# Expert blocks fed from a DRAM scratch: the row gather per block replaced by one scatter, reads per block, and two combining pairs moved

## The chip, the cores and the metric

The kernel runs on 1 core of one Trainium2 chip. The metric is the device time of one execution in microseconds (us). Engines: PE is TensorE (matmuls; its weight loads are shown as PEld), DVE is VectorE, ACT is ScalarE, POOL is GpSimd, SP is SyncE. A name with q (SPq, POOLq) is an engine's sequencer, the part that issues DMAs and waits. All transfers of the core are carried by 16 DMA engines.

## The reference, cut to what matters

A two-layer step of a model on 288 tokens (256 of a prompt, 32 samples), width 1024, all float32. Each layer mixes tokens (retention heads and a causal convolution) and then runs a mixture of 16 experts, two per token. The change is in the second part:

```python
def grouped_moe(h, w_router, b_router, w_gate, w_up, w_down):
    ...
    wts, local = lax.top_k(cand, TOP_K)            # two experts per token
    wts = wts / jnp.sum(wts, axis=-1, keepdims=True)
    ...
    xs = h_pad[slot_tok].reshape(n_blocks, MOE_BLOCK, D)   # rows of the tokens of each block
    def block_ffn(args):
        xb, e = args
        return (jax.nn.silu(xb @ w_gate[e]) * (xb @ w_up[e])) @ w_down[e]
    ys = lax.map(block_ffn, (xs, block_e)).reshape(cap, D)
    ys = (ys * slot_w[:, None]).astype(h.dtype)
    return jnp.zeros((N + 1, D), h.dtype).at[slot_tok].add(ys)[:N]
```

## The kernel before, in words

**Weights.** Every large weight is streamed once through `ring`, 12 units of 1 MB (L129, `NSLOT`). SP issues the loads in one fixed order. Before each it waits on `freed[s]`, after each the data raises `loaded[s]`. An expert needs exactly 12 units: four of gate, four of up, four of down (L349 to L357). So unit s of expert e+1 is loaded as soon as the last block of expert e has used unit s.

**Blocks.** The tokens of an expert are taken in blocks of 64 slots (`BLK`). An expert with more than 64 assigned tokens runs two blocks (`nsubi`, the inner loop L731), and only its last block lets the ring go on, since `freed` is compared with the count of all blocks. With this data there are 35 blocks for 32 experts: 18 in layer 0, 17 in layer 1.

**One block on PE** (L729 to L788): eight gate products (`half_products`, from `xg`, the transposed rows of the block) with the three combining pairs 0 to 2 of the block before set between k = 3 and k = 4 (`combine`, which writes the block's weighted results back to token order into PSUM); eight up products with pair 3 after k = 0; then `gather`, which picks the rows of the next block out of `h2tok` (288 tokens, in SBUF) by a product with a 0/1 matrix `sel`; the transposes of the hidden row `hs`; the transposes of `selw`; the transposes of the gathered rows `xtok`; then eight down products.

**The other engines.** DVE builds `selw` and `sel` per block (L1388 to L1402), adds what each pair combined to `xT` (`take`, L1377), multiplies gate and up (L1408, L1414), and copies `h2T` and `selT` out of PSUM. ACT takes the sigmoid of the gate, copies the gathered rows (`xtok`, L960), the transposed rows (`xg`, L962) and the result (`ysb`, L965). POOL does nothing between L1546 and L1547, that is during all blocks of a layer.

**Before the first block** of a layer the router runs on DVE (L1285 to L1364, its last result is `slots`, the slot of each token), and the rows of block 0 are gathered on PE from `slot0`, which is known earlier. After the last block come the next layer's first modulation products, whose weights follow the experts' in the ring.

Of the kernel before, what the change touches and what calls it, by code (L numbers as in the profile page):

```python
# [11 lines left out]
T = SEQ + NS  # L12
P = 128
# [8 lines left out]
BLK = 64  # L22
MAXSUB = -(-T // BLK)

MAXBLK = E + (2 * T) // BLK
NC = 1 + B
# [90 lines left out]
def hybrid_step_kernel(nc, x_prompt, x_sample, state_ret, state_conv, c_prompt, c_sample, w_mod, b_mod, g_mix_norm,  # L117
# [6 lines left out]
    with ctx:  # L124
# [20 lines left out]
        nsubi = sb("nsubi", [P, E + 1], i32)  # L145
        rtmp = sb("rtmp", [P, KC, NS])
# [78 lines left out]
        sel1 = cut("moe", 3, BLK)  # L225
# [10 lines left out]
        PAIR_BANKS = ((6, 7), (0, 5), (1, 4), (0, 5))  # L236
# [3 lines left out]
        def sem(name):  # L240
# [4 lines left out]
        in_first, in_const, in_x, in_c, in_rows, in_taps, in_wr = (sem(n) for n in (  # L245
            "in_first", "in_const", "in_x", "in_c", "in_rows", "in_taps", "in_wr"))
        (cpad, cond_step, x_trans, x_copied, x_squared, rows_trans, rows_copied, mod_done, mod_evac,
         fold_done) = (sem(n) for n in (
             "cpad", "cond_step", "x_trans", "x_copied", "x_squared", "rows_trans", "rows_copied",
             "mod_done", "mod_evac", "fold_done"))  # L250
        mix_open, moe_open, y_out, fin_cp = (sem(n) for n in ("mix_open", "moe_open", "y_out", "fin_cp"))
        cb_loaded, routed, x_summed = sem("cb_loaded"), sem("routed"), sem("x_summed")
        tick = sem("tick")
# [7 lines left out]
        dchain pchain sel0_ready g0_done x0_copied gt0_done  # L261
        mod2_done mod2_evac mod2_fold mod2_added""".split()
        moe_names = """sel_ready gathered xrow_copied xg_trans xg_copied
# [13 lines left out]
        fin_rs, fin_y, fin_tr, fin_cd = V.var_ready, V.h_ready, V.h2_trans, V.x_mid  # L277
# [16 lines left out]
        def _(sp):  # L294
# [76 lines left out]
            yp = y_prompt[0].rearrange("(r p) d -> p r d", p=P)  # L371
            sp.wait_ge(fin_cp, 2)
# [11 lines left out]
        def _(pe):  # L384
# [7 lines left out]
            taken = pe.alloc_register("chunks_taken")  # L392
            for s in range(NSLOT):
                pe.sem_inc(freed[s], 1)
# [49 lines left out]
            for j in range(2):  # L444
                mod_slab(j, j, lambda s: 16)
                pe.drain().then_inc(mod_done, 1)
                if j == 0:
                    pe.wait_ge(in_taps, 16)
# [5 lines left out]
                mod_turn(2 + j, modS[:, j, :]).then_inc(fold_done, 1)  # L454
            pe.wait_ge(in_wr, 32)

            for l in range(L):
# [256 lines left out]
                def combine(j):  # L714
                    for hf in range(2):
                        last = mm(ps[:, PAIR_BANKS[j][hf], 0:T], ysb[hf * 64:hf * 64 + 64, j * P:(j + 1) * P],
                                  selT[hf * 64:hf * 64 + 64, :], True, True)
                    return last
# [9 lines left out]
                pe.reg_mov(taken, 2)  # L728
# [845 lines left out]
```

## Time and profile before

| | us |
|---|---|
| median of 3 runs | 1494.03 |
| lowest, highest | 1492.83, 1499.04 |
| the profiled execution | 1498.92 |
| its span | 1497.0 |
| PE busy | 1425.7 (95%) |
| DVE busy | 678.9 (45%) |
| ACT busy | 239.8 (16%) |
| POOL busy | 104.7 (7%) |
| moved by the DMA engines | 501.93 MB, mean 335 GB/s |

The page cuts the span into 40 slices of 37.4 us; a digit is a busy share in tenths. The windows view gives the same for any stretch: engine, busy us, in brackets the number of instructions, then PE's granted clock (1.00 is 2.4 GHz), the DMA engines' share and GB/s. A share of 1.03 is what the profiler shows when all 16 DMA engines never rest. PE's busy time counts modelled ends of matmuls, so short waits between matmuls do not show in it; where PE waits is read from gaps in the timeline.

### The profile page before, as it was taken

Reading aid. Unit: us, or ns where it says so; the run is one execution under the profiler, and the core shown is the slowest. Engines: PE = TensorE matmul, PEld = TensorE weight load, DVE = VectorE, ACT = ScalarE, POOL = GpSimd, SP = SyncE. Lnnn points to the kernel's source line nnn. Section 1 sums busy time; section 2 is a strip of 40 time slices with the busy share of each in tenths; the row PEclk is TensorE's granted clock in tenths of the full one; section 3 lists DMA queues with packets and bytes.
Section 4 is the critical chain, followed back from the end, with each engine's and each line's share of the span. In section 5 each row is a group of like instructions: output and inputs, shape, how many; then the busy total and the mean of one; then the engine's idle time right before and its main releaser. Section 6 shows DMA issues by size and latency. Waiting matters only on the chain.

```text
span 1497.0 us, 19640 instructions
## 1 busy us (share of the span) xinstructions
PE 1425.7 (95%) x6993; PEld 660.9 (44%) x6994; DVE 678.9 (45%) x1986; ACT 239.8 (16%) x392; POOL 104.7 (7%) x149
## 2 busy tenths in 40 slices
PE   6999998999999999999989999989999999999996
PEld 3777664333333233333337766633333323333333
DVE  2697646333333333333347965553343323234333
ACT  1201311111110111111131123211111101111112
POOL 1071111000000000000001611100000000000000
PEclk9899996999999999999999999989999999999998
DMA  9944558999999974999998355589999999799992
GB/s 332 355 159 148 226 219 312 393 410 409 409 410 410 410 302 159 391 410 410 409 409 341 132 202 228 211 328 410 410 410 409 410 410 409 308 397 410 410 409 76
DMA packets 131314, 501.93 MB, mean 335 GB/s; under 512 B 8635, under 2 KB 8955, under 8 KB 131266
## 3 DMA queue, kind: packets, MB, share of 16 engines
q1 hardware_dynamic: 127056, 487.84, 82.7%
q0 software_dynamic: 3600, 11.21, 2.3%
q10 hardware_dynamic: 626, 2.46, 0.6%
q8 instruction: 20, 0.33, 0.1%
q14 instruction: 12, 0.10, 0.0%
HBM read 495.32 MB, written 7.00 MB: 336 GB/s over the span
## 4 chain that ended last, share of the span: by engine, by line
PE 62%; SPq 24%; DMA 5%; DVE 4%; issue 3%; ACT 1%; PEld 0%; PEldq 0%; ACTq 0%; DVEq 0%
PE ps L386 58%; SPq L356 21%; PE ps L389 3%; DMA ring<-in_w_mod 3%; DMA ring<-in_w_exp_up 2%; SPq L368 1%; DVE arena L1017 1%; SPq L311 1%; ACT arena L829 1%; SPq L359 0%; PEld ps L386 0%; ACT L829 0%; ACT hT L829 0%; DVE hT L1224 0%; DVE rt L1279 0%
## 5 line engine op out<-in xcount | busy, mean ns | idle before, releaser
L386 PE MATMUL ps<-ring,arena 128*64 128x512 f32 x3360 | 754.6, 599 | 17.5 <-DMA ring<-in_w_exp_up 12.9
L386 PEld LDWEIGHTS ps<-ring,arena 128*64 128x64 f32 x3360 | 233.0, 137 | 479.7 <-issue 425.5
L829 ACT ACTIVATE arena<-ps 128x512 f32<-128x512 f32 (+3 forms) x240 | 129.8, 551 | 831.3 <-PE ps L386 742.8
L386 PE MATMUL ps<-hT,ring 128*128 128x288 f32 x1024 | 256.2, 412 | 7.1 <-DVE hT L1091 4.2
L1380 DVE SCALAR_TENSOR_TENSOR xT<-ps,mod,xT 128x256 f32<-128x256 f32 x280 | 133.0, 475 | 254.8 <-PE ps L386 254.8
L386 PE MATMUL ps<-arena 64*128 64x288 f32 (+6 forms) x1212 | 234.1, 485 | 10.6 <-DVE arena L1347 4.7
L386 PEld LDWEIGHTS ps<-hT,ring 128*128 128x128 f32 x1024 | 196.7, 193 | 64.9 <-DVE hT L1091 4.7
L386 PEld LDWEIGHTS ps<-arena 64*128 64x128 f32 (+6 forms) x1212 | 99.8, 167 | 161.9 <-issue 145.6
L1122 DVE SCALAR_TENSOR_TENSOR arena<-arena,wcT 128x256 f32<-128x256 f32 x240 | 123.6, 577 | 1.6
L829 ACT ACT_TABLE_LOAD x49 | 62.9, 1283 | 314.7 <-PE ps L386 292.3
L1414 DVE TENSOR_TENSOR arena<-ps,arena 128x512 f32<-128x512 f32 x35 | 24.2, 691 | 163.1 <-PE ps L386 163.1
L389 PE MATMUL ps<-cst,arena 128*128 128x128 f32 (+5 forms) x533 | 83.0, 289 | 12.7 <-DVE arena L1004 7.2
L389 PEld LDWEIGHTS ps<-cst,arena 128*128 128x128 f32 (+5 forms) x533 | 60.2, 145 | 59.6 <-issue 47.1
L1408 DVE TENSOR_TENSOR arena<-ps,arena 128x512 f32<-128x512 f32 x35 | 24.2, 691 | 123.5 <-ACT arena L829 123.5
L1416 DVE COPY arena<-ps 128x512 f32<-128x512 f32 x35 | 24.2, 691 | 87.3 <-PE ps L389 87.3
L386 PE MATMUL ps<-ring,condT 128*32 128x512 f32 x384 | 44.8, 597 | 7.0 <-DMA ring<-in_w_mod 6.9
L1382 DVE TENSOR_TENSOR rtmp<-ps,rtmp 128x32 f32<-128x32 f32 x280 | 50.2, 179 | 0.0
L1467 POOL DMA_DIRECT2D out<-in_state_conv x2 | 1.1, 542 | 581.3 <-DVE hT L1091 539.8
L1493 POOL TENSOR_TENSOR arena<-arena,wcT 128x128 f32<-128x128 f32 x62 | 33.5, 572 | 62.3 <-DVE arena L1108 61.8
L1388 DVE TENSOR_SCALAR arena<-cst,slots,wts 128x128 f32<-128x128 f32 x105 | 29.8, 341 | 0.9 <-issue 0.9
L1390 DVE TENSOR_SCALAR arena<-cst,slots,wts 128x128 f32<-128x128 f32 x105 | 30.0, 343 | 0.0
L386 PEld LDWEIGHTS ps<-ring,condT 128*32 128x32 f32 x384 | 11.0, 109 | 34.4 <-issue 22.3
(169 smaller groups left out, 578.5 us busy)
## 6 DMA issues: line engine op xcount, KB each, us to landing
ring<-in_w_exp_gate SPq DMA_DIRECT2D x128, 1024.0 KB, 16.6
ring<-in_w_exp_up SPq DMA_DIRECT2D x128, 1024.0 KB, 17.7
ring<-in_w_exp_down SPq DMA_DIRECT2D x128, 1024.0 KB, 17.5
ring<-in_w_mod SPq DMA_DIRECT2D x48, 1024.0 KB, 8.8
ring<-in_w_in SPq DMA_DIRECT2D x24, 1024.0 KB, 21.5
ring<-in_w_out SPq DMA_DIRECT2D x8, 1024.0 KB, 12.8
big<-in_state_ret POOLq DMA_DIRECT2D x4, 512.0 KB, 10.4
arena<-in_state_ret POOLq DMA_DIRECT2D x4, 512.0 KB, 5.2
```

Of the source, the lines that this page charges most:

```text
L356: sp.dma_start(ring[:, s], exp_v[j][bass.ds(l * E + e, 1), q] .rearrange("a p k c -> (a p) k c")).then_inc(loaded[s], 16)
L386: return nc.tensor.matmul(out, lhsT, rhs, start=start, stop=stop, skip_group_check=True)
L389: return nc.tensor.transpose(out, in_, ident[0:n, 0:n])
L829: return nc.scalar.activation(out, in_, f, **kw)
L1122: ins = v.scalar_tensor_tensor(cT[:, ct, 0:SEQ], src, wcol, cT[:, ct, 0:SEQ], ALU.mult, ALU.add)
L1380: v.scalar_tensor_tensor(xT[:, c, 0:SEQ], ps[:, bank, 0:SEQ], mod[:, M_GT2 + c, 0:1], xT[:, c, 0:SEQ], ALU.mult, ALU.add)
L1382: last = v.tensor_tensor(rtmp[:, c, :], ps[:, bank, SEQ:T], rtmp[:, c, :], ALU.add)
L1388: v.tensor_scalar(selw[:, t, :], iota, slots[:, 0, t:t + 1], wts[:, 0, t:t + 1], ALU.is_equal, ALU.mult)
L1390: last = v.tensor_scalar(selw1[:, t, :], iota, slots[:, 1, t:t + 1], wts[:, 1, t:t + 1], ALU.is_equal, ALU.mult)
L1408: v.tensor_tensor(hs, ps[:, 2, :], gs, ALU.mult).then_inc(V.gated, 1)
L1414: v.tensor_tensor(hs, ps[:, 3, :], hs, ALU.mult).then_inc(V.h_act, 1)
L1493: last = gp.tensor_tensor(slot[:, k].rearrange("p c (b t) -> p c b t", b=B), win[:, :, :, tap:tap + T_DEC], wc[:, tap * CT:(tap + 1) * CT] ...
```

## The change

- A DRAM tensor `block_rows` of 1664 rows of 1024 float32 (`xrows`) is added. In layer 0 POOL writes zeros to all of it, out of `qm`, which DVE has cleared; DVE waits for that before it writes `qm`.
- Once per layer, as soon as `slots` is known, POOL scatters the 288 rows of `h2tok` to their slots, once for each of the two experts of a token: six indirect DMAs, 2 x 288 rows of 4 KB.
- Per block POOL reads the rows of the next block, 64 x 1024, into `xtok` with two DMAs of 64 x 512 (128 KB each). The read for block n+2 is issued when PE has transposed the rows of block n+1.
- The gather on PE, the `sel` matrices on DVE and the copy of the gathered rows on ACT are gone from the block loop. Block 0 is still gathered on PE.
- PE's order in a block is new: pairs 2 and 3 are combined after the transposes of `hs`, just ahead of the down products, in PSUM banks (5, 7) and (2, 3). At a block's end PE waits until DVE has taken all four pairs.
- POOL's load of the next layer's convolution history (L1537) now stands behind the scatter. Some semaphores are merged or reused.
- The number of unit buffers (12) and the order of the weight loads do not change.

```diff
+        rowi = sb("rowi", [P, 2, 3], i32)
+        xrows = nc.dram_tensor("block_rows", (XROWS, D), f32, kind="Internal").ap()
...
-        PAIR_BANKS = ((6, 7), (0, 5), (1, 4), (0, 5))
+        PAIR_BANKS = ((6, 7), (0, 5), (5, 7), (2, 3))
+        LAST_BANKS = ((6, 7), (0, 5), (1, 4), (0, 5))
...
# PE, block loop
-                                for j in range(3):
+                                for j in range(2):
                                     combine(j).then_inc(V.comb_done, 1)
...
-                            if k == 0:
-                                pe.wait_ge(V.comb_used, taken)
-                                combine(3).then_inc(V.comb_done, 1)
                         last.then_inc(V.up_done, 1)
-                        pe.wait_ge(V.sel_ready, nn)
-                        pe.reg_add(taken, taken, 1)
+                        pe.reg_add(got, got, 32)
+                        pe.wait_ge(V.rows_in, got)
+                        transposes(1, xtok).then_inc(V.xg_trans, 1)
+                        pe.wait_ge(V.selw_ready, nn)
+                        pe.reg_add(taken, taken, 2)
                         pe.wait_ge(V.comb_used, taken)
-                        gather().then_inc(V.gathered, 1)
-                        pe.wait_ge(V.h_act, nn)
-                        transposes(4, hs).then_inc(V.trans_done, 1)
-                        pe.wait_ge(V.selw_ready, nn)
                         for t, (t0, m) in enumerate(TILES):
                             last = tr(ps[:, 6, t0:t0 + m], selw[0:m, t, :], m)
                         last.then_inc(V.selT_done, 1)
-                        pe.wait_ge(V.xrow_copied, nn)
-                        transposes(1, xtok).then_inc(V.xg_trans, 1)
+                        pe.wait_ge(V.h_act, nn)
+                        transposes(4, hs).then_inc(V.trans_done, 1)
+                        for j in range(2, 4):
+                            combine(j).then_inc(V.comb_done, 1)
...
                         last.then_inc(V.down_done, 1)
+                        pe.reg_add(taken, taken, 2)
+                        pe.wait_ge(V.comb_used, taken)
# ACT, block loop
-                    act.wait_ge(V.gathered, n + 1)
-                    a(xtok, ps[:, 1, :]).then_inc(V.xrow_copied, 1)
# DVE
+                if l == 0:
+                    dve.wait_ge(rows_zeroed, 16)
...
+                v.tensor_copy(rowi[:, :, :], slots[:, :, :]).then_inc(V.rowi_ready, 1)
...
-                    for t in range(3):
-                        v.tensor_scalar(sel[:, t, :], iota[:, 0:BLK], slots[:, 0, t:t + 1], None, ALU.is_equal)
-                    for t in range(3):
-                        last = v.tensor_scalar(sel1[:, t, :], iota[:, 0:BLK], slots[:, 1, t:t + 1], None, ALU.is_equal)
...
-                    v.tensor_tensor(sel[:, :, :], sel[:, :, :], sel1[:, :, :], ALU.add).then_inc(V.sel_ready, 1)
# POOL
+                if l == 0:
+                    zeros = qm[:, :, :].rearrange("p h w -> p (h w)")
+                    pool.dma_start(xrows.rearrange("(p r) d -> p r d", p=P),
+                                   zeros.unsqueeze(1).to_broadcast([P, XROWS // P, D])).then_inc(rows_zeroed, 16)
...
+                pool.wait_ge(V.h2_copied, 6)
+                pool.wait_ge(V.rowi_ready, 1)
+                for t, (t0, m) in enumerate(TILES):
+                    for k in range(2):
+                        gp.indirect_dma_start(xrows[:, :], bass.IndirectOffsetOnAxis(ap=rowi[0:m, k, t:t + 1], axis=0),
+                                              h2tok[0:m, t, :], None).then_inc(rows_out, 16)
+                pool.wait_ge(rows_out, 96 * (l + 1))
+                pool.wait_ge(V.gt0_done, 1)
+
+                def read_rows(r0):
+                    for nh in range(2):
+                        pool.dma_start(xtok[nh * BLK:(nh + 1) * BLK, :], xrows[bass.ds(r0, BLK), nh * 512:nh * 512 + 512]) \
+                            .then_inc(V.rows_in, 16)
+
+                read_rows(BLK)
                 pool.wait_ge(V.sf_stored, 16)
...
                 pool.drain().then_inc(mix_open, 1)
+                nb = pool.value_load(nsubi[0:1, E:E + 1], min_val=E, max_val=MAXBLK)
+                with pool.Fori(1, nb) as n:
+                    pool.wait_ge(V.xg_trans, n)
+                    pool.sem_inc(tick, 1)
+                    read_rows(n * BLK + BLK)
```

PE in the block loop, from the last up products (a `ring` row is weights, `cst` rows are transposes) to the down products. Before:

```order
L386 MATMUL ps<-ring,arena 64x512 [waits unit_loaded7]
L386 MATMUL ps<-ring,arena 64x512 x3
L765 REGISTER_ALU [waits sel_ready]
L386 MATMUL ps<-arena 64x512 [waits comb_used]
L386 MATMUL ps<-arena 64x512 x5
L389 MATMUL ps<-cst,arena 128x128 [waits h_act]
L389 MATMUL ps<-cst,arena 128x128 x3
L389 MATMUL ps<-cst,arena 128x128 [waits selw_ready]
...
L389 MATMUL ps<-cst,arena 128x128 [waits xrow_copied]
L389 MATMUL ps<-cst,arena 128x128 x3
L778 REGISTER_ALU [waits hT_copied]
```

And after the change (line numbers are higher by 5):

```order
L391 MATMUL ps<-ring,arena 64x512 [waits unit_loaded7]
L391 MATMUL ps<-ring,arena 64x512 x3
L768 REGISTER_ALU
L394 MATMUL ps<-cst,arena 128x128 [waits rows_in]
L394 MATMUL ps<-cst,arena 128x128 x3
L772 REGISTER_ALU [waits selw_ready]
...
L394 MATMUL ps<-cst,arena 128x128 [waits h_act]
L394 MATMUL ps<-cst,arena 128x128 x3
L391 MATMUL ps<-arena 128x288 x4
L391 MATMUL ps<-ring,arena 64x512 [waits unit_loaded8,hT_copied]
```

The six gather products are gone, four combining products stand in front of the wait for `hT_copied`, and the wait for `rows_in` is new.

POOL from the last stores of the states to the end of a layer's blocks, before:

```order
L1521 DMA out<-arena 128x4x128
L1528 TENSOR_TENSOR arena<-arena,cst 32x1024 x4
L1533 DMA out<-arena 128x8x128 x2
L1533 DMA out<-big 128x8x128 x2
L1537 DMA arena<-in_state_conv 120x2x512
L1545 ISA
L1551 ISA
```

And after:

```order
L1537 DMA out<-big 128x8x128 x2
L1545 DMA block_rows<-arena,rowi 1664x1024 x6
L1552 DMA arena<-block_rows 64x512 x2
L1558 DMA arena<-in_state_conv 120x2x512
L1566 ISA
L1568 TENSOR_LOAD nsubi
L1568 ISA x2
L1569 UNCONDITIONAL_BRANCH
L1552 ISA
L1552 DMA arena<-block_rows 64x512
L1552 ISA
L1552 DMA arena<-block_rows 64x512
```

The history load now comes after the scatter and the first read, and the last two DMAs repeat in a loop over the blocks.

## Rows read from the trace of the kernel before

**Rows 1.** The page's slices: share of the DMA engines and GB/s.
```profile
DMA  9944558999999974999998355589999999799992
GB/s 332 355 159 148 226 219 312 393 410 409 409 410 410 410 302 159 391 410 410 409 409 341 132 202 228 211 328 410 410 410 409 410 410 409 308 397 410 410 409 76
```

**Rows 2.** Windows (stretch; busy us and instructions by engine; clock, DMA share, GB/s).
```profile
452.00:483.00 31.00, 28.90 (x141) 9.81 (x139) 10.33 (x37) 3.67 (x5) 0.00 (x0) 1.00 1.03 410
...
535.00:540.00 5.00, 5.00 (x26) 1.67 (x24) 1.01 (x6) 0.57 (x1) 0.00 (x0) 1.00 0.02 8
...
590.00:595.00 5.00, 5.00 (x26) 1.64 (x22) 1.44 (x8) 0.12 (x1) 0.00 (x0) 1.00 0.00 0
...
1300.00:1305.00 5.00, 5.00 (x26) 1.66 (x24) 1.88 (x9) 0.00 (x0) 0.00 (x0) 1.00 0.02 10
...
1460.00:1465.00 5.00, 5.00 (x29) 2.06 (x27) 2.03 (x4) 1.05 (x2) 0.00 (x0) 1.00 0.74 295
```

**Rows 3.** Timeline of PE, down to down (start us, us, engine, line, operation, count).
```profile
532.20 10.52 PE L386 MATMUL ps<-ring,arena 128*64 128x512 f32 x48
542.65 1.73 PE L386 MATMUL ps<-arena 64*128 64x288 f32 x12
...
548.75 0.76 PE L386 MATMUL ps<-arena 64*128 64x288 f32 x4
...
555.49 2.89 PE L386 MATMUL ps<-arena 128*64 128x512 f32 x12
558.32 1.63 PE L389 MATMUL ps<-cst,arena 128*128 128x128 f32 x11
559.93 10.52 PE L386 MATMUL ps<-ring,arena 128*64 128x512 f32 x48
```

**Rows 4.** Timeline, PE and DVE between up and down of layer 0's block 0.
```profile
269.33 2.89 PE L386 MATMUL ps<-arena 128*64 128x512 f32 x12
269.66 0.69 DVE L1414 TENSOR_TENSOR arena<-ps,arena 128x512 f32<-128x512 f32 x1 [4.14 <-PE ps L386]
...
272.15 1.64 PE L389 MATMUL ps<-cst,arena 128*128 128x128 f32 x11
...
272.85 0.69 DVE L1416 COPY arena<-ps 128x512 f32<-128x512 f32 x1 [2.49 <-PE ps L389]
```

**Rows 5.** Timeline of SP: weight loads issued again after each of the two pauses.
```profile
541.25 7.37 SPq L356 DMA_DIRECT2D ring<-in_w_exp_gate  x4
...
596.71 2.08 SPq L356 DMA_DIRECT2D ring<-in_w_exp_gate  x2
```

**Rows 6.** Timeline of PE, last down products of layer 1, then the last combining.
```profile
1464.48 7.09 PE L386 MATMUL ps<-ring,arena 128*64 128x512 f32 x32
1472.36 1.73 PE L386 MATMUL ps<-arena 64*128 64x288 f32 x12 [0.79 <-ACT arena L829]
```

**Rows 7.** DMA queues: packets, MB, share; 330 to 500, 1490 to 1497, 225 to 255.
```profile
q1 hardware_dynamic: 18067, 69.64, 102.6%
...
q1 hardware_dynamic: 608, 1.18, 49.0%
...
q0 software_dynamic: 720, 2.59, 24.3%
```

**Rows 8.** Windows at the first block of layer 0.
```profile
250.00:255.00 5.00, 3.81 (x11) 1.21 (x12) 3.70 (x15) 0.60 (x1) 0.00 (x0) 0.66 0.02 3
```

**Rows 9.** Timeline, POOL's history load and DVE's last step for `slots`, layer 0.
```profile
242.69 0.77 POOL L1537 DMA_DIRECT2D arena<-in_state_conv  x1
...
247.46 0.20 DVE L1364 TENSOR_REDUCE slots<-rt 128x3 f32<-128x48 f32 x1
```

**Rows 10.** Timeline, POOL's first convolution work and DVE's write to `qm`, layer 0.
```profile
79.30 4.34 POOL L1493 TENSOR_TENSOR arena<-arena,wcT 128x128 f32<-128x128 f32 x8 [30.34 <-DVE arena L1108]
...
135.37 0.27 DVE L1159 TENSOR_TENSOR qm<-arena,cst 128x112 f32<-128x112 f32 x1
```

**Rows 11.** Windows, first modulation products, PE fed by DMA.
```profile
22.00:30.00 8.00, 6.74 (x45) 2.59 (x43) 2.41 (x2) 0.60 (x1) 0.00 (x0) 1.00 1.02 409
```

More of the change, by code:

```diff
@@ L25 @@
 MAXBLK = E + (2 * T) // BLK
+XROWS = -(-(MAXBLK + 1) * BLK // P) * P
 NC = 1 + B
@@ L712, in half_products, with combine @@
                     return last
-                def combine(j):
+                def combine(j, banks=PAIR_BANKS):
                     for hf in range(2):
-                        last = mm(ps[:, PAIR_BANKS[j][hf], 0:T], ysb[hf * 64:hf * 64 + 64, j * P:(j + 1) * P],
+                        last = mm(ps[:, banks[j][hf], 0:T], ysb[hf * 64:hf * 64 + 64, j * P:(j + 1) * P],
                                   selT[hf * 64:hf * 64 + 64, :], True, True)
@@ L727, in _ @@
                 pe.reg_mov(nn, 0)
-                pe.reg_mov(taken, 2)
+                pe.reg_mov(taken, 0)
+                pe.reg_mov(got, 0)
                 with pe.Fori(0, E) as e:
@@ L1391, in _ @@
                     last.then_inc(V.bchain, 1)
-                    dve.wait_ge(V.bchain, n * 3 + 1)
+                    dve.wait_ge(V.bchain, n * 2 + 1)
                     v.tensor_tensor(selw[:, :, :], selw[:, :, :], selw1[:, :, :], ALU.add).then_inc(V.selw_ready, 1)
                     v.tensor_scalar(slots[:, :, :], slots[:, :, :], -float(BLK), None, ALU.add).then_inc(V.bchain, 1)
-                    dve.wait_ge(V.bchain, n * 3 + 2)
-                    for t in range(3):
-                        v.tensor_scalar(sel[:, t, :], iota[:, 0:BLK], slots[:, 0, t:t + 1], None, ALU.is_equal)
-                    for t in range(3):
-                        last = v.tensor_scalar(sel1[:, t, :], iota[:, 0:BLK], slots[:, 1, t:t + 1], None, ALU.is_equal)
-                    last.then_inc(V.bchain, 1)
-                    dve.wait_ge(V.bchain, n * 3 + 3)
-                    v.tensor_tensor(sel[:, :, :], sel[:, :, :], sel1[:, :, :], ALU.add).then_inc(V.sel_ready, 1)
-                    for j in range(3):
+                    for j in range(2):
                         dve.wait_ge(V.comb_done, n * 4 + j + 1)
@@ L1408, in _ @@
                     v.tensor_tensor(hs, ps[:, 2, :], gs, ALU.mult).then_inc(V.gated, 1)
-                    dve.wait_ge(V.comb_done, n * 4 + 4)
-                    take(3)
                     dve.wait_ge(V.up_done, n + 1)
@@ L1416, in _ @@
                     v.tensor_copy(h2T, ps[:, 4, :]).then_inc(V.hT_copied, 1)
+                    for j in range(2, 4):
+                        dve.wait_ge(V.comb_done, n * 4 + j + 1)
+                        take(j)
                     dve.wait_ge(V.selT_done, n + 1)
+                    dve.wait_ge(V.bchain, n * 2 + 2)
                     v.tensor_copy(selT, ps[:, 6, 0:T]).then_inc(V.selT_copied, 1)
```

62 lines of the change are left out of this document (32 added, 30 removed).

## The prediction, as put on record before the result was known

> **What bounds the kernel now.** First the page's slices [rows 1]: from slice 8 to 13, 17 to 20, 27 to 33 and 36 to 38 the DMA engines move 409 to 410 GB/s, flat. These are the expert blocks. Flat means that the DMA engines are the limit: an expert is 12 MB, 12.58e6 bytes / 410 GB/s = 30.7 us. Then the windows [rows 2]: in 452 to 483 the DMA share is 1.03 while PE still has 2.1 us of gaps in 31. Then PE's timeline where it never waits for data [rows 3]: from one start of the down products (532.20) to the next (559.93) a block takes 27.73 us. So an expert with one block costs PE 27.7 us and the DMA engines 30.7, and PE waits. Only where an expert has two blocks does PE lead: during its first block nothing is freed, the ring fills and the DMA engines stop. The windows show three such pauses [rows 2]: at 535 to 540 and at 590 to 595 in layer 0 (two such experts in succession), at 1300 to 1305 in layer 1. SP's loads restart at 541.25 and 596.71 [rows 5], 55.46 us apart, exactly 2 x 27.73: the second pause ends when PE has done two whole blocks. At the end of layer 1 the last weight byte lands at about 1463.6 (share 0.74 of 1460 to 1465 [rows 2]) and PE is done with down at 1464.48 + 7.09 = 1471.6 [rows 6], 8.0 us behind. Layer 0 ends in DMA-bound loads for the next layer, so there PE's lag is worth nothing.
>
> So the sum has two sides: less PE time counts only in the pauses and at the end; more bytes count everywhere else.
>
> **PE's block.** Removed: the gather, 2.89 us, 12 records (6 products) [rows 3]. But the gather also covered DVE's `h_act`. After up ends (269.33), DVE starts at +0.33, takes 0.69; the transposes of `hs` can begin at about +1.1, last some 0.6 (11 transposes take 1.63), and DVE's copy starts 0.70 after their start and takes 0.69 [rows 4]. In the new order the transposes of `xtok` and `selw` (7 of 11, 1.0 us) fill the wait for `h_act`, and pairs 2 and 3 (8 records, by 1.73 us for 12 records: 1.15, or 0.76 for one pair twice: 1.5; I take 1.4) fill the copy. Up to down becomes 1.1 + 0.6 + 1.4 = 3.1 us, where it was 559.93 - 555.49 = 4.44: 1.34 less. The gate and up parts lose pairs 2 and 3: 0.58 + 0.76 = 1.34 less. A block is 27.73 - 2.68 = 25.0 us. The new wait at the block's end (for DVE's takes of pairs 2 and 3, eight short operations) lies beside the down products (7.09 us [rows 6]); the new wait for `rows_in` has 25 us from issue to need after block 0. DVE and ACT lose work off the path: nothing.
>
> **What that buys.** Pause 1: PE reaches the first freed unit 1.3 us earlier: -1.3. Pause 2: two blocks of 25.0 in place of 27.73: -5.5. Layer 1's pause: -1.3. End of layer 1: PE is now DMA-fed (25.0 against over 31), so it ends a quarter of down (7.09 / 4 = 1.8) behind the last byte in place of 8.0: -6.2. In each layer's first block the ring is refilled at PE's pace; a faster block gives about 1 us each: -2.0. Sum -16.3 us.
>
> **The reads per block.** 64 x 1024 x 4 = 0.262 MB in pieces of 2 KB. The trace has no such read from POOL's queue; the nearest rows [rows 7]: 1.18 MB stored in 2 KB pieces took 49% of 7 us on 16 engines = 54.9 engine-us, so 12.2 for 0.262 MB, 0.76 us. POOL's queue moved 2.59 MB in 24.3% of 30 us: 116.6 engine-us, so 11.8, 0.74 us. Lower end: bytes at the ring's 410 GB/s, 0.64. Upper end: each 2 KB piece costs what a ring packet costs, 102.6% x 170 x 16 / 18067 = 0.154 us, x 128 / 16 = 1.24 us. I take 0.75, since two rows agree. Of 35 reads 5 are free: the one issued in each layer's block 0, where PE's pace refills the ring, the two issued before layer 0's second pause, whose end PE sets, and the last, when all weights are in. So 30 are paid: +22.5 us (19.2 to 37).
>
> **The scatter.** 2 x 288 rows of 4 KB = 2.36 MB per layer; at POOL's price (45 engine-us per MB) 6.6 us of all engines. It starts when `slots` is done, 247.7 [rows 9]. From 250 to 255 the DMA engines rest (share 0.02 [rows 8]) and the ring's loads flow again from about 257. Six issues at 0.77 us, the price of a direct one [rows 9], are 4.6 us; indirect ones are not in the trace. I take it that most fits and 1.5 us per layer is paid: +3.0 (0 to 13). The history load, 0.49 MB, moves from before the rest to behind it, layer 0 only: +1.2. The first read is then issued near 260 and has until 269.3, when block 0 ends up [rows 4].
>
> **The zeroes.** 1664 x 4 KB = 6.8 MB, 17 us of all engines at 410 GB/s, 19 at POOL's price, issued where POOL's wait of 30.34 us begins, at 49 [rows 10]. Slices 2 to 5 are at 148 to 226 GB/s [rows 1], so even behind all that the ring loads before 75 us the zeroes are down by 94. POOL's next work is at 79.30 and DVE writes `qm` at 135.37 [rows 10], over 40 us later. Cost 0; without that cover up to 19.
>
> **Sum.** -16.3 + 22.5 + 3.0 + 1.2 = +10.4 us on the profiled 1498.92 (span 1497.0 plus 1.9 around it). That execution is 4.9 above the median of the runs, 1494.03; the same +10.4 on the median gives 1504.4 us.
>
> **Rivals.** (A) *The reads ride along for nothing, and the kernel is faster.* If the ring's 410 GB/s is held back by SP's own queue and not by the engines, a second queue finds gaps. Then 22.5 is dropped: 1504.4 - 22.5 = 1481.9. The sign turns where a read costs (22.5 - 10.4) / 30 = 0.40 us. Against it: the share of 1.03 leaves no gap on any engine [rows 2]. Chance 0.16.
>
> (B) *A read costs its packets*, 1.24 us: + 30 x 0.49 = 14.7, 1519. The ring's packets are twice as long, and the stores in 2 KB pieces came at half a packet's price, so I doubt it. Chance 0.11.
>
> (C) *The scatter is late.* If an indirect issue takes 3 us, the last leaves POOL at 266, all 6.6 us of it meets the ring's loads, and the first read lands near 274 where PE wants it at 269.3: per layer 5 more of scatter and some 2.5 of stall that the ring's queue doesn't cover, 1504.4 + 15 = 1519. The Trainium skill (SBUF — State Buffer, "Who interferes with whom") has a rule for this: copies of DVE in certain modes keep GpSimd from writing the descriptors of its own DMAs until they end. By that rule the scatter and the reads would be late while DVE is busy; in the trace POOL issues next to a busy DVE at 0.77 us each [rows 9], which doesn't show it. Chance 0.07.
>
> (D) *PE's block doesn't shrink by 2.7* because the chain h_act, transposes, copy has no cover left: with half of it, + 7, 1511. Chance 0.04.
>
> (E) *PE's clock falls.* PE will wait about 6 us of 31 in short gaps. If that took the granted clock to the lower of its two levels (1.2 of 2.4 GHz) for a part of each block, +30 or more. In 22 to 30 PE was busy 6.74 of 8 us, fed by DMA, at clock 1.00 [rows 11]. The Trainium skill (TensorE: Matmul & The Clock Gate, "HAM oscillation — how this bites in real kernels") tells of a kernel in which waiting for DMA between short groups of matmuls halved the clock each time; by it the time could be over 1530. Chance 0.03.
>
> **How the numbers follow.** Forecast 1504.4 (reads 0.64 to 0.85, scatter 0 to 4 a layer: 1494 to 1511), chance 0.54; A 0.16; B 0.11; C 0.07; D 0.04; E 0.03; several small gains at once, within 0.5% of before, 0.05. A measurement of this kernel tells 0.5% (7.5 us) from no change. Slower by more: 0.34 of the forecast's 0.54, B, C, 0.03 of D, E: 0.58. Within: 0.19 of the forecast, the small gains, 0.01 of D: 0.25. Faster: A and 0.01: 0.17. For eight in ten the range leaves out A and E: 1489 to 1519, the lower end for a forecast with the cheaper reads, no scatter cost and a few us more saved in the pauses.
>
> **What would show it.** PE down to down near 25.0 us after each pause; DMA share still 1.03 with about 410 GB/s in the fed stretches, and an expert's period there of about 31.4 us in place of 30.7; POOL's queue with some 9 MB more; the second pause of layer 0 shorter by 5.5; PE's last down ending 1.8 us behind the last byte. Wrong if the period stays 30.7 (A), exceeds 31.8 (B), if PE waits for `rows_in` or for POOL in block 0 (C), if the block is 26 us or more (D), or if the clock is below 1.00 in the fed stretches (E).

## The result

The changed kernel takes 1533.7 us (median of 4 runs, 1529.5 to 1534.88). The kernel before, run beside it, takes 1495.62 us. The ratio is 1.0249, with a 95% interval of 1.0217 to 1.028: slower by 37 us. The forecast was 1504.4 us with a range up to 1519, so the sign came out as forecast and the size did not: the time lies 15 us above the upper end.

The profiled execution took 1532.98 us, 34.1 more than that of before (1498.92). First the page of the changed kernel. It has lines of part 1 (busy), part 2 (40 slices of 38.3 us), part 3 (queues), part 5 (groups) and part 6 (issues).

```profile
PE 1360.0 (89%) x6573; PEld 620.3 (41%) x6574; DVE 632.3 (41%) x1743; ACT 219.2 (14%) x357; POOL 154.2 (10%) x232
DMA  9974659999999986999998265599999999999993
GB/s 339 405 287 156 231 194 370 372 403 402 402 395 402 402 314 228 391 397 403 402 415 339 111 235 232 214 341 402 400 398 402 403 403 402 353 358 395 401 404 150
q1 hardware_dynamic: 127056, 487.84, 81.7%
q0 software_dynamic: 9984, 31.92, 6.1%
...
L1552 POOL DMA_DIRECT2D arena<-block_rows x70 | 36.9, 528 | 897.3 <-PE ps L394 859.7
...
arena<-block_rows POOLq DMA_DIRECT2D x70, 128.0 KB, 6.0
```

PE lost 66 us of work (1425.7 before), yet the kernel is slower. In the expert stretches most slices show 395 to 404 GB/s, where it was 409 to 410 [rows 1]. Their share is as high as ever. So they are not idle for longer: they are busy for the same time with fewer bytes. POOL's queue (q0) moved 20.7 MB more than before: 9.2 of reads, 4.7 of scatter and 6.8 of zeroes. The "some 9 MB" of the prediction counted the reads alone.

The stages, read from the timelines of both kernels (start of the first gate products of a layer, SP's restarts after its pauses, start of the last combining), show where the time goes:

| stretch | before, us | after, us | difference |
|---|---|---|---|
| layer 0, first gate products to restart after pause 1 | 290.0 | 306.8 | +16.8 |
| pause 1 to pause 2 (two whole blocks) | 55.5 | 49.6 | -5.9 |
| pause 2 to the start of layer 1 | 186.1 | 190.6 | +4.5 |
| layer 1 up to its first gate products | 202.4 | 206.6 | +4.2 |
| layer 1, first gate products to restart after the pause | 321.9 | 336.2 | +14.3 |
| restart to the last combining | 165.2 | 166.8 | +1.6 |

These add up to +35.5. The start (+0.4) and the end behind the last combining (-1.7) make it the +34.3 of the spans. The +4.2 comes without the change too: see the last but one bullet of "Why the prediction was wrong".

What was to be gained was gained; what had to be paid was dearer. Here is the gain first: SP's restarts in layer 0 (as [rows 5]), then PE's timeline from the end of pause 1 on (as [rows 3]).

```profile
558.52 6.88 SPq L360 DMA_DIRECT2D ring<-in_w_exp_gate  x4
...
608.13 6.87 SPq L360 DMA_DIRECT2D ring<-in_w_exp_gate  x4
```

```profile
571.53 1.63 PE L394 MATMUL ps<-cst,arena 128*128 128x128 f32 x11
573.09 1.24 PE L391 MATMUL ps<-arena 64*128 64x288 f32 x8
574.26 10.52 PE L391 MATMUL ps<-ring,arena 128*64 128x512 f32 x48
584.72 1.24 PE L391 MATMUL ps<-arena 64*128 64x288 f32 x8
585.89 10.52 PE L391 MATMUL ps<-ring,arena 128*64 128x512 f32 x48
596.34 1.63 PE L394 MATMUL ps<-cst,arena 128*128 128x128 f32 x11
597.90 1.24 PE L391 MATMUL ps<-arena 64*128 64x288 f32 x8
```

From pairs 2 and 3 (573.09) to the same place (597.90) a block takes 24.81 us, where it was 27.73 and 25.0 was forecast. The 11 transposes stand in one piece without a wait. The two restarts are 49.61 us apart: two blocks.

Now the price. SP's issues of the down weights in a stretch that the DMA engines feed, of the changed kernel, and the same stretch in windows, of the changed kernel and then of the one before:

```profile
365.60 11.44 SPq L360 DMA_DIRECT2D ring<-in_w_exp_down  x4
399.02 8.70 SPq L360 DMA_DIRECT2D ring<-in_w_exp_down  x4
429.71 11.44 SPq L360 DMA_DIRECT2D ring<-in_w_exp_down  x4
```

```profile
370.00:500.00 130.00, 108.50 (x504) 34.56 (x502) 36.44 (x119) 12.30 (x16) 4.19 (x8) 1.00 1.03 401
```

```profile
370.00:500.00 130.00, 125.90 (x603) 43.41 (x600) 43.79 (x152) 16.59 (x23) 0.00 (x0) 1.00 1.03 410
```

The pattern repeats after two experts: (429.71 - 365.60) / 2 = 32.06 us for one. Without the reads it is 30.72 (below). Each read takes 1.34 us from the weights, not the 0.75 of my sum. The DMA view of the same stretch (slices of 3.25 us) shows where:

```profile
GB/s 406 413 411 406 408 415 321 408 410 410 411 406 413 411 405 413 321 411 406 411 413 406 408 412 410 405 323 412 412 406 412 410 407 412 411 387 343 405 415 411
q1 hardware_dynamic: 13248, 51.06, 99.8%
q0 software_dynamic: 384, 1.05, 2.9%
```

All slices are near 410 but those in which a read lands: 321, 321, 323, and the pair 387 and 343. The four reads take 2.9% of 130 us, 0.94 us each, where their bytes (1.05 MB) would take 2.0% at 410 GB/s. The dip and the price are the same thing: 410 - 321 = 89 GB/s less for 3.25 us are 0.29 MB, or 0.70 us at 410 GB/s, and the read's own bytes are 0.64 us more: 1.34. The two queues' shares, 99.8% and 2.9%, add up to 102.7%, as much as the 102.6% that the weights alone took before [rows 7]: no engine rests, but they move less while a read lands.

Two smaller things. POOL's timeline at the scatter, and PE's at the end of the first block of layer 0:

```profile
249.68 1.05 POOL L1545 DMA_INDIRECT block_rows<-arena,rowi  x1 [5.95 <-DVE rowi L1370]
251.04 0.99 POOL L1545 DMA_INDIRECT block_rows<-arena,rowi  x1 [0.30 <-issue]
...
256.04 0.86 POOL L1545 DMA_INDIRECT block_rows<-arena,rowi  x1 [0.30 <-issue]
262.77 1.15 POOL L1552 DMA_DIRECT2D arena<-block_rows  x2 [5.86 <-DMA block_rows<-arena,rowi]
```

```profile
270.91 2.09 PE L394 MATMUL ps<-cst,arena 128*128 128x128 f32 x11 [2.42 <-DMA arena<-block_rows]
```

An indirect issue takes 0.86 to 1.05 us with 0.30 between: about 1.3 us each, where I had 0.77 and no gap. So the first read is issued at 262.8, not near 260, and PE waits 2.42 us for it. In layer 1 the same wait is 1.59 us.

After the 2.42 us PE's clock is down for a moment. Timeline of PE and window:

```profile
272.94 2.29 PE L391 MATMUL ps<-arena 64*128 64x288 f32 x8
```

```profile
270.00:275.00 5.00, 4.09 (x19) 2.67 (x19) 1.37 (x4) 0.60 (x1) 0.00 (x0) 0.69 1.02 295
```

The 11 transposes take 2.09 us in place of 1.63 and the two pairs 2.29 in place of 1.24: 1.5 us more.

### The profile page after: what moved, and what is told of

It is laid out like the page before. It is cut to its first block, busy times and chain, and to the rows that moved or that the text cites. A ratio compares the mean times of both kernels' runs of the same rounds, so it can differ in the third digit from the quotient of the medians.

```text
span 1531.3 us, 18921 instructions
## 1 busy us (share of the span) xinstructions
PE 1360.0 (89%) x6573; PEld 620.3 (41%) x6574; DVE 632.3 (41%) x1743; ACT 219.2 (14%) x357; POOL 154.2 (10%) x232
## 4 chain that ended last, share of the span: by engine, by line
SPq 45%; PE 34%; DMA 8%; DVE 5%; issue 5%; ACT 2%; PEld 1%; POOL 1%; PEldq 1%; ACTq 0%; POOLq 0%; DVEq 0%
SPq L360 42%; PE ps L391 31%; DMA ring<-in_w_exp_down 4%; DMA ring<-in_w_mod 2%; PE ps L394 2%; SPq L372 1%; DVE arena L1020 1%; DMA arena<-block_rows 1%; DMA block_rows<-arena,rowi 1%; SPq L315 1%; PEld ps L391 1%; SPq L363 1%; POOL block_rows L1545 1%; ACT hT L834 1%; ACT L834 0%
## 5 line engine op out<-in xcount | busy, mean ns | idle before, releaser
L391 PE MATMUL ps<-ring,arena 128*64 128x512 f32 x3360 | 779.0, 602 | 110.3 <-DMA ring<-in_w_exp_up 52.3
L391 PEld LDWEIGHTS ps<-ring,arena 128*64 128x64 f32 x3360 | 219.2, 137 | 634.4 <-issue 349.7
L834 ACT ACTIVATE arena<-ps 128x512 f32<-128x512 f32 (+4 forms) x205 | 109.0, 543 | 866.8 <-PE ps L391 540.1
L391 PE MATMUL ps<-arena 64*128 64x288 f32 (+3 forms) x792 | 134.9, 428 | 10.3 <-DVE arena L1352 4.5
L1552 POOL DMA_DIRECT2D arena<-block_rows x70 | 36.9, 528 | 897.3 <-PE ps L394 859.7
L391 PEld LDWEIGHTS ps<-arena 64*128 64x128 f32 (+3 forms) x792 | 73.4, 185 | 71.2 <-issue 55.8
L391 PE MATMUL ps<-ring,condT 128*32 128x512 f32 x384 | 49.5, 646 | 10.1 <-DMA ring<-in_w_mod 10.0
L391 PEld LDWEIGHTS ps<-ring,condT 128*32 128x32 f32 x384 | 11.2, 115 | 41.9 <-issue 22.7
## 6 DMA issues: line engine op xcount, KB each, us to landing
block_rows<-qm POOLq DMA_DIRECT2D x1, 6656.0 KB, 43.2
```

Source lines behind the costliest of these rows:

```text
L391: return nc.tensor.matmul(out, lhsT, rhs, start=start, stop=stop, skip_group_check=True)
L834: return nc.scalar.activation(out, in_, f, **kw)
L1552: pool.dma_start(xtok[nh * BLK:(nh + 1) * BLK, :], xrows[bass.ds(r0, BLK), nh * 512:nh * 512 + 512]) \
```

## The experiments

Why does a read cost 1.34 us? Theory at the start: the price is in how the read is made (pieces of 2 KB, two DMAs, POOL's queue, or where it lands). All times below are beside a kernel before of 1497 to 1499 us. An expert's time is half the distance of two of SP's issues as above. Every kernel but the two marked computes the whole result.

**No reads at all.** (Marked.) The reads and PE's wait for them are left out; `xtok` keeps old rows, so this is a price and no kernel.

```diff
-                    for nh in range(2):
-                        pool.dma_start(xtok[nh * BLK:(nh + 1) * BLK, :], ...)
+                    return
-                        pe.wait_ge(V.rows_in, got)
```

> The changed kernel without the reads per block (zeroes, scatter and the new order on PE stay; every block after the first computes on the rows of block 0, so the values are not the reference's; two final semaphores get numbers of their own). In the changed kernel an expert's period where the weights set the pace is 32.05 us (SP's down loads at 365.60 and 429.71, two experts), before it was 30.7. Theory R, the reads cost about 1.35 us each and are the slowdown: the period is 30.7 again and the time falls by about 30 x 1.35 = 40 us to 1493. Rival S, the scatter and the first block's stall cost much of it: the time stays above 1505. Rival P, PE's new order costs: the period stays near 32.

Measured: 1478.58 us, ratio 0.9859 [0.9815, 0.9903]; an expert takes (421.30 - 359.86) / 2 = 30.72 us. That is 14 us under the 1493 expected. Its wrong rows changed the routing of layer 1: 34 blocks in place of 35, and no pause there, which flatters it, by how much wasn't measured. Layer 0 has its 18 blocks as before and can be compared. From the first gate load of its second expert to the first of layer 1, SP takes 666.92 us before, 683.59 after the change, 663.00 without the reads. The terms of the sum for this stretch without the reads (-1.3, -5.5, -1.0, +1.5, +1.2) make -5.1; measured is -3.9. So in layer 0 the rest of the sum holds no cost above about 1 us that I missed, and an expert without a read takes what it took before (30.7): nearly all of the loss is in the reads.

**One DMA over all 128 partitions.** The same bytes in the same 2 KB pieces, but partition 2r + n gets half n of row r. ACT's copy of the transposed rows (not shown) puts the columns back in order; so does that of the kernels below in which the tile's rows lie in this order.

```diff
-                    for nh in range(2):
-                        pool.dma_start(xtok[nh * BLK:(nh + 1) * BLK, :], xrows[bass.ds(r0, BLK), nh * 512:nh * 512 + 512])
+                    pool.dma_start(xtok[:, :], xrows[bass.ds(r0, BLK), :].rearrange("r (n c) -> (r n) c", n=2))
```

> Each block's rows are read by one DMA onto all 128 partitions (row halves side by side, ACT's copy of the transposed rows puts them in order) in place of two DMAs onto 64 partitions; the pieces stay at 2 KB, the bytes the same. Theory of the half set: writing to 64 partitions only, or two DMAs in place of one, is what makes a read cost 1.35 us of all engines in place of 0.75: the period falls to about 31.4 and the time to about 1515. Rival, the price is in the bytes or the 2 KB pieces or POOL's queue: period 32.0, time 1533.

Measured: 1506.78 us, ratio 1.0054 [1.0033, 1.0075], 31.32 us per expert: 0.60 for a read. Its DMA view of 370 to 500:

```profile
GB/s 407 408 415 408 413 408 408 412 410 408 410 412 407 416 410 407 412 408 408 412 410 408 407 417 410 411 407 410 412 408 408 412 410 412 412 407 411 411 407 408
q1 hardware_dynamic: 13555, 52.25, 100.6%
q0 software_dynamic: 320, 1.05, 2.0%
```

No slice dips, and a read now costs its bytes at 410 GB/s. That gives back 27 us by the medians (1533.7 - 1506.78), 22 of them by the reads (30 x 0.74). Of the rest, 4.6 us lie ahead of layer 0's first block in the traces (its second expert's first load is at 250.87 in place of 255.43), where the two kernels do the same work: that start moves by some us from one execution to the next. The run leaves open which of three things did it: one DMA in place of two, the spread over partitions, or other sizes.

**Pieces of 4 KB, one DMA, onto partitions 0 to 63.** PE transposes eight pieces of 64 rows in place of four of 128 (not shown).

```diff
-                    for nh in range(2):
-                        pool.dma_start(xtok[nh * BLK:(nh + 1) * BLK, :], ...)
+                    pool.dma_start(xtok2[0:BLK, :], xrows[bass.ds(r0, BLK), :])
```

> Each block's rows are read by one DMA onto 64 partitions in pieces of 4 KB in place of two DMAs in pieces of 2 KB (PE transposes eight 64-row pieces in place of four 128-row ones). Theory of the pieces or of the number of DMAs: period 31.4, time about 1515. Theory of the half set of partitions: period stays at 32.0, time about 1533. Bytes or queue: also 32.0.

Measured: 1530.27 us, ratio 1.0232 [1.0182, 1.0282], (426.75 - 362.68) / 2 = 32.04 us per expert: 1.32 for a read. One DMA with half as many pieces is as dear as two.

**The same two DMAs from ACT's queue,** issued behind ACT's copy of the transposed rows.

```diff
-                        pool.dma_start(xtok[nh * BLK:(nh + 1) * BLK, :], ...)
+                            act.dma_start(xtok[nh * BLK:(nh + 1) * BLK, :], ...)
```

> The same two reads per block, issued from ACT's queue in place of POOL's (after ACT's copy of the transposed rows). Theory of the queue, that DMAs from POOL's software queue cost the engines more: period about 31.4, time about 1515. Rival, the queue doesn't matter: 32.0 and about 1533.

Measured: 1528.54 us, ratio 1.0202 [1.016, 1.0245], 31.96 us per expert: 1.24 for a read. The queue has little to do with it. Theory had been that POOL's queue costs more; it would have given 1515.

**Two DMAs of 64 partitions, every second one.**

```diff
-                        pool.dma_start(xtok[nh * BLK:(nh + 1) * BLK, :], ...)
+                        pool.dma_start(xtok[nh:P:2, :], ...)
```

> As the changed kernel, two DMAs of 64 x 512 per block, POOL's queue, pieces of 2 KB; only the destination differs: each DMA writes every second partition over all 128 in place of the lower or the upper 64 (ACT puts the columns in order). One DMA onto 128 partitions brought the fed period from 32.05 to 31.32 us and the time to 1507. Theory G, what costs is that a DMA's destination lies in one half of the partitions: period 31.3 to 31.4, time 1507 to 1510. Rival N, what costs is the number of DMAs or of partitions in one DMA: period stays at 32.0, time 1530.

Measured: 1504.7 us, ratio 1.0062 [1.004, 1.0083], (420.38 - 357.75) / 2 = 31.32 us per expert: 0.60. Two DMAs, 64 partitions each, 2 KB pieces: all as in the changed kernel. Only the place of the partitions differs (and the order in ACT's copy), and the price is more than halved. So the cause is that each DMA lands on one run of 64 neighbouring partitions.

**Useless extra reads** on top of the one-DMA kernel, the same 0.262 MB per block each time, into a spare tile. First onto 128 partitions, then onto 0 to 31 (8 KB each):

```diff
+                    pool.dma_start(xspare[:, :], xrows[...].rearrange("r (n c) -> (r n) c", n=2))
```

> The version with one 128-partition read per block, plus a second equal read of 0.262 MB into an unused tile. Control for the next one. Both theories: each read costs 0.62 us of period (31.32 less 30.7), so the period is 31.9 to 32.0 and the time 1507 + 30 x 0.62 = 1526.

```diff
+                    pool.dma_start(xspare[0:32, :], xrows[...].rearrange("(p r) c -> p (r c)", r=2))
```

> The same version, plus a read of the same 0.262 MB into 32 partitions (8 KB in each). Theory G, a price set by how few of the partitions take the data: 128 partitions 0.62 us, 64 partitions 1.34, so 32 partitions some 2.6: period 33.9, time 1507 + 30 x 2.6 = 1585. Rival N, a price for anything but a full 128-partition DMA, whatever the number: 1.34, period 32.7, time 1547. Rival B, bytes alone: 31.9, time 1526.

Measured: 1524.87 us (ratio 1.018 [1.0158, 1.0202]) and 31.94 per expert, 0.61 for the extra read; and 1556.34 us (1.0391 [1.0373, 1.0409]) and (434.48 - 368.94) / 2 = 32.77, 1.45 for it. The second was a miss for the theory as I had it then: 32 partitions should have cost 2.6, twice the 64, if each partition had its own share of the bandwidth. They cost hardly more than 64.

So partitions seem to share something in groups. The Trainium skill (SBUF — State Buffer, "Door 1: The DMA port swizzle") says how: there are 16 DMA ports of 8 partitions; which one a partition is on depends on its number modulo 32 in steps of four and on whether it is under 64, so that 0 and 32 share one, and 64 and 96 another. By that page of the Trainium skill 0 to 31 and 0 to 63 both reach 8 ports, 64 to 127 the other 8, and every second or every fourth partition all 16. Two runs test it, with 32 partitions and 8 KB in each; the edits are against the kernel with 0 to 31:

```diff
-                    pool.dma_start(xspare[0:32, :], ...)
+                    pool.dma_start(xspare[0:P:4, :], ...)
```

> The one-DMA version onto all 128 partitions (1506.8 us, 31.32 us per expert), with a second, useless read of the same 0.262 MB for each block, onto 32 partitions that lie apart (0, 4, 8, ... 124), 8 KB each. The same read onto partitions 0 to 31 gave 32.80 us per expert, 1.48 more. Theory H (the price follows how the destination lies over the partitions): 0.6 more, 31.9 per expert, total about 1525, as with the second read onto 128. Theory N (few partitions or 8 KB pieces are dear): 1.48 more again, 32.8, 1556. The Trainium skill (SBUF — State Buffer, "Door 1: The DMA port swizzle") gives partitions 0 to 31 and 0 to 63 alike only half of the DMA ports, and every fourth partition of the 128 all of them; that is theory H.

```diff
-                    pool.dma_start(xspare[0:32, :], ...)
+                    for g in range(2):
+                        pool.dma_start(xspare[32 * g:32 * g + 16, :], xrows[bass.ds(r0 + 32 * g, 32), :]...)
```

> The same, with the useless read onto partitions 0 to 15 and 32 to 47, in two DMAs of 16 partitions, again 32 partitions with 8 KB each. If the price followed the number of partitions or the pieces, it would be as with 0 to 31: 1.48 more, 32.8 per expert, 1556. If two partitions 32 apart share what limits them, these 32 have half as many ways in as 0 to 31: twice the price, 2.4 to 3.0 more, 33.7 to 34.3 per expert, total 1585 to 1605. The Trainium skill (SBUF — State Buffer, "Door 1: The DMA port swizzle") puts these 32 partitions on 4 ports and 0 to 31 on 8; by its 27.2 GB/s for a port the read takes 2.4 us (an estimate from the page).

Measured: 1524.0 us, ratio 1.0185 [1.0156, 1.0213], and 1595.59 us, ratio 1.0652 [1.0626, 1.0679]. SP's issues and the slices of 370 to 500, first with 0, 4, ... 124, then with 0 to 15 and 32 to 47:

```profile
363.04 11.20 SPq L361 DMA_DIRECT2D ring<-in_w_exp_down  x4
...
426.92 11.21 SPq L361 DMA_DIRECT2D ring<-in_w_exp_down  x4
```

```profile
GB/s 408 410 412 407 410 415 412 408 410 410 411 410 408 411 411 415 410 410 410 410 407 412 410 408 411 416 410 412 406 412 411 407 411 410 410 417 408 408 411 411
```

```profile
375.38 10.94 SPq L361 DMA_DIRECT2D ring<-in_w_exp_down  x4
...
443.65 10.94 SPq L361 DMA_DIRECT2D ring<-in_w_exp_down  x4
```

```profile
GB/s 396 407 405 416 408 406 412 411 407 304 250 408 408 408 413 407 408 413 408 422 146 389 410 407 410 413 407 408 413 408 309 279 412 408 406 416 407 406 415 408
```

31.94 and 34.14 us per expert: the extra read costs 0.62 and 2.81 us. Same bytes, same 8 KB in each partition, same number of partitions; only which ones (and two DMAs of 16 partitions in place of one in the last). Two issues of SP are few, so I read the prices a second time, in layer 1, from SP's first gate load for its fifth expert to that for its eleventh: (1289.60 - 1097.47) / 6 = 32.02 us per expert in the changed kernel, 30.72 without reads, 31.33 in the one-DMA kernel. The prices side by side:

| destination | DMAs | per partition | price of 0.262 MB | the same in layer 1 |
|---|---|---|---|---|
| all 128 | 1 | 2 KB | 0.60, 0.61 | 0.61, 0.61 |
| every second | 2 | 2 KB | 0.60 | 0.60 |
| every fourth | 1 | 8 KB | 0.62 | 0.62 |
| 0 to 63, then 64 to 127 (the change) | 2 | 2 KB | 1.34 | 1.30 |
| the same from ACT's queue | 2 | 2 KB | 1.24 | 1.27 |
| 0 to 63 | 1 | 4 KB | 1.32 | 1.43 |
| 0 to 31 | 1 | 8 KB | 1.45 | 1.44 |
| 0 to 15 and 32 to 47 | 2 | 8 KB | 2.81 | 2.52 |

So the narrow prices are known to about 0.1 us, the last to 0.3, and the three groups stand far apart. Which port a byte goes through stands in no row: the map is the Trainium skill's, and the runs show that the price follows it.

An estimate from the 27.2 GB/s for a port on that page of the Trainium skill is 0.60, 1.20 and 2.41 us for 16, 8 and 4 ports; the rows agree at 16 ports and lie 3 to 20% above it at 8 and 4. That the two DMAs of the changed kernel touch both halves does not help: the two cost what one onto 0 to 63 costs with the same bytes, as if they ran one behind the other.

**Half of each read** (marked: only the first 512 columns; the other half of `xtok` is old).

```diff
-                    for nh in range(2):
+                    for nh in range(1):
```

> The changed kernel with only the first of the two DMAs of each read (512 of 1024 columns, onto partitions 0 to 63); the other half of xtok keeps old data, so the output is wrong in those columns and the routing of layer 1 may differ. 35 blocks as before unless it does. If a read's price is its two DMAs one after the other, each onto one half of the partitions (theory H): half the price goes, 31.4 per expert in place of 32.05, total about 1533.7 - 20 = 1514. If a read has a fixed price whatever it carries: 32.0 and no change.

Measured: 1506.55 us, ratio 1.0062 [1.0041, 1.0083]; (422.84 - 359.85) / 2 = 31.50 us per expert, 0.78 for 0.131 MB, where 0.67 would be half; over the six experts of layer 1 it is 0.67. The price goes with the bytes, with a small fixed part at most. It still has 35 blocks. The total fell by 27 us where 20 were expected. In the two traces 21 us of it lie in the expert blocks and behind them, where the reads give 30 x 0.67 = 20; 5 us lie ahead of the first blocks (2.5 in each layer), where nothing is read.

**A second scatter** in each layer, of the same rows into another scratch, behind the first read, in the one-DMA kernel.

```diff
                 read_rows(BLK)
+                for t, (t0, m) in enumerate(TILES):
+                    for k in range(2):
+                        gp.indirect_dma_start(xrows2[:, :], ..., h2tok[0:m, t, :], None).then_inc(rows_out, 16)
```

> The one-DMA version, with a second scatter of the same rows into another scratch in each layer, issued by POOL behind the first read. It leaves nothing out. My sum put a scatter at 1.5 us per layer, 3 in all, with an upper end of 13. The second one meets the ring's loads in full, so it shows the upper end: 2.36 MB per layer at 410 GB/s are 5.8 us, two layers 11.5, total about 1518. If rows of a scatter onto DRAM cost more than their bytes, as the 64-partition reads do: 20 or more, over 1527. If it costs under 5 us, the scatter can't explain any of the miss.

Measured: 1517.37 us, ratio 1.0141 [1.0107, 1.0174], 10.6 us over the one-DMA kernel by the medians and 13 by the ratios: 5.3 to 6.5 a layer. In the traces SP's way from the second expert's first load to the restart after the (first) pause is 5.3 us longer in layer 0 and 5.8 in layer 1. That is its bytes at 410 GB/s (5.8), and no extra for being indirect shows. It is a price for a scatter that meets the ring in full. The first one lies partly in time in which the DMA engines rested before [rows 8]; it was not run by itself. With the history load it cost about 3.9 in layer 0 (the -3.9 above, less the -7.8 of PE's terms), where I had 2.7.

**The combining pairs alone**, in the kernel before, with the gather kept. All four pairs are waited for at the block's end, as in the change.

```diff
-        PAIR_BANKS = ((6, 7), (0, 5), (1, 4), (0, 5))
+        PAIR_BANKS = ((6, 7), (0, 5), (5, 7), (2, 3))
-                                for j in range(3):
+                                for j in range(2):
```

> The kernel before, with only the two combining pairs moved (pairs 2 and 3 ahead of the down products, new banks, wait for all four pairs at the block's end); gather, sel matrices and ACT's copy stay, no scratch. Theory: PE's block stays near 27.7 us, since the middle grows by 1.4 and gate and up shrink by 1.34, and the time stays within 3 us of before. Rival: the move alone costs (the wait at the block's end, the banks): block 28.5 us or more, time over 1505.

Measured: 1498.88 us, ratio 0.9987 [0.9969, 1.0005]: no change. Where PE sets the pace a block takes 27.53 us, 0.20 less than before and 2.7 more than after the change. So the shorter block comes almost wholly with the removal of the gather. What the removal would give with the pairs left where they were was not run.

## Why the prediction was wrong

- **What bounds the kernel: right.** Fed stretches are set by the DMA engines, pauses and the end by PE; the table of stretches shows both signs.
- **PE's block: right.** 24.81 us for 25.0. No wait is left between the pairs and the down products, so the pairs do fill the time of the copy of `h2T`.
- **Pauses: right.** 55.46 - 49.61 = 5.85 for 5.5 at pause 2.
- **The end of layer 1: right in kind, 1.6 us too good.** PE's timeline there, to set beside [rows 6], and the window:

```profile
1500.03 5.37 PE L391 MATMUL ps<-ring,arena 128*64 128x512 f32 x24
1505.61 1.94 PE L391 MATMUL ps<-ring,arena 128*64 128x512 f32 x8 [0.21 <-DMA ring<-in_w_exp_down]
1508.33 1.73 PE L391 MATMUL ps<-arena 64*128 64x288 f32 x12 [0.78 <-ACT arena L834]
```

```profile
1500.00:1505.00 5.00, 5.00 (x26) 1.64 (x24) 2.92 (x11) 0.00 (x0) 0.00 (x0) 1.00 0.85 338
```

  PE waits for the last unit and does a quarter of down behind it, not a whole one. But the last byte lands near 1504.1 (share 0.85 of 1500 to 1505), and PE is released at 1505.61 and done at 1507.5: 3.4 us behind the byte, where I had 1.8. The gain is 8.0 - 3.4 = 4.6 in place of 6.2.
- **The reads: this step failed.** "I take 0.75, since two rows agree" and its upper bound of 1.24 came from rows of stores, of POOL's queue and of the ring [rows 7], none of them a transfer that lands on half of the partitions alone. I argued from the size of the pieces, which plays no part that shows: on 64 neighbouring partitions the pieces of 4 KB cost as much as those of 2 KB, and 8 KB on every fourth partition cost no more than 2 KB on all. The runs put 1.34 in its place, above that bound: 30 x (1.34 - 0.75) = 17.7 us of the miss. Rival B had nearly the price (1519), and its sign, over 31.8 us per expert, came true; but its mechanism, a price by the packet, is not there. I cited the Trainium skill's page SBUF — State Buffer for another rule, while "Door 1: The DMA port swizzle" on the same page bore on the change. An estimate by it, 1.20 us, would have made the sum 1517.9.
- **The scatter: too cheap in its issue.** Six issues took 7.2 us, not 4.6, and the first read came late: waits of 2.42 and 1.59 us in the two first blocks. That is the start of rival C, without DVE in it: the issues are 1.2 to 1.4 us apart. C's 3 us for an issue did not show.
- **The zeroes: right.** Issued at 49.32, they took 43.2 us to land. So they were down by 94, over 40 us before DVE needs `qm` [rows 10], and POOL's next work starts at 79.55 (79.30 before).
- **The sum again**, with 1.34: -16.3 + 40.2 + 3.0 + 1.2 = +28.1; with the two waits +32.1. Against it stand +34.1 in the profiled executions and +37 (32 to 42) by the ratio. Three more terms were wrong or missing: the last read is not free, since it is issued at 1466.75 and the weights land until 1504 (+1.3); the clock in layer 0's first block (+1.5); the end of layer 1 (+1.6). All in, it is +36.5, near the ratio's +37. But the profiled +34.1 contains the +4.2 of the next bullet, and against the rest the sum is now some 7 us too high: that it comes so near the ratio is partly luck. Waits in the first blocks can be caught up later, where the DMA engines set the pace; how much of them was paid was not measured. For the one-DMA kernel, with 0.60 and without the waits: -16.3 + 18.0 + 4.2 = +5.9, against +8.1 (4.9 to 11.2) by the ratio.
- **Layer 1 ahead of its first block: not shown to be the change.** That stretch took 202.4 us before, 206.6 after, and 207.4 in the kernel with the pairs alone, which has neither scatter nor read. In three other variants it took 207.4, 203.3 and 202.3 (the one-DMA kernel, the one with every second partition, the one with the extra read onto 128). So it differs by up to 5 us among kernels that do the same work there. Windows of the router part show PE at a granted clock of 0.80 before and 0.65 after:

```profile
959.00:985.00 26.00, 20.19 (x108) 12.53 (x104) 21.87 (x96) 9.48 (x19) 3.60 (x4) 0.80 1.01 397
```

```profile
976.00:1005.00 29.00, 25.48 (x108) 16.24 (x104) 22.27 (x97) 9.65 (x19) 5.21 (x6) 0.65 0.92 360
```

  Why it differs was not settled.
- **Rivals.** A (free reads) is out: even the cheapest read costs its bytes. D is out by PE's block. E is out for this kernel's fed stretches, where the clock is 1.00; only in layer 0's first block did it show, for 1.5 us.

No variant that computes the whole result beat the kernel before. The best with reads, spread over the partitions, is 0.5% slower: reads that cost their bytes, 30 x 0.60 = 18 us, still outweigh what PE's shorter block brings (16 us by the forecast, 15 with the end of layer 1 as measured).

## What to carry to other kernels

Where the DMA engines set the time, price a transfer by its bytes and by where it lands: a tile on a run of 64 partitions, or 32, took 2.0 to 2.4 times from the other transfers what the same bytes take when spread over all 128, and an access pattern of every second partition was enough to avoid that. Look for the price of a new transfer in a row with the same shape on the SBUF side, and where there is none, put the upper end at twice the bytes at least. Work that is moved from an engine with slack to the one resource without any was paid in full here, while what it freed paid only in the pauses and at the end.

## What the runs showed of the hardware

The 16 engines stay at a share of 1.03 while less is moved (390 GB/s in 370 to 500 with the 4-port read, 410 before): the share doesn't tell a slowed transfer from a full one, only GB/s does.

And PE's clock fell after some waits. With the read at 2.81 us, PE waits 3.67 us at a time for a down unit. Timeline and windows of that kernel:

```profile
396.77 5.37 PE L392 MATMUL ps<-ring,arena 128*64 128x512 f32 x24
405.82 7.92 PE L392 MATMUL ps<-ring,arena 128*64 128x512 f32 x24 [3.67 <-DMA ring<-in_w_exp_down]
```

```profile
395.00:405.00 10.00, 7.14 (x37) 2.73 (x36) 5.28 (x18) 0.81 (x1) 1.54 (x3) 0.96 1.03 321
405.00:415.00 10.00, 9.18 (x34) 3.05 (x36) 0.53 (x3) 0.60 (x1) 0.00 (x0) 0.70 1.02 408
```

After the wait as many records of the same kind, 24, take 7.92 us in place of 5.37, and the granted clock of those 10 us is 0.70, so the lower level of 1.2 GHz for a part of them. In the changed kernel the wait at that place is 1.51 us, and the clock stays at 1.00. Yet in layer 0's first block it fell to 0.69 after a wait of 2.42 us, and in the one-DMA kernel to 0.72 (265 to 270) after one of 1.63, both behind 10.5 us of matmuls without a gap. So the length of the wait alone does not tell. This is rival E, in a kernel where it hardly matters, since the DMA engines set the pace there. The Trainium skill (TensorE: Matmul & The Clock Gate, "HAM oscillation — how this bites in real kernels") tells of a kernel whose waits for DMA put PE on the lower clock each time. The trace agrees: 0.70 behind the wait of 3.67 us.
